# Probabilities scaled on ScalarE before the transposes, and value products in groups of four, in a fused two-block kernel

## The reference

```python
s = jnp.einsum('bqgrd,bqkgd->bqgrk', qg, kg).astype(jnp.float32) * scale
s = jnp.where(valid[:, :, None, None, :], s, -jnp.inf)
p = jax.nn.softmax(s, axis=-1).astype(v.dtype)
o = jnp.einsum('bqgrk,bqkgd->bqgrd', p, vg)
...
a = dsa_attention(q, k, v, qi, ki, wi, k_sel) * jax.nn.silu(z_a)
```

## Time and profile before

| what | us |
|---|---|
| median of the 3 runs | 3760.19 (3759.91 to 3761.3) |
| profiled execution, its own time | 3762.86 |
| its span in the trace | 3761.1 |
| first transposes of the stage | 1229.2 |
| last gate multiplication of the stage | 1679.03 |

### The profile page before, as it was taken

How to read it: one execution, slowest core, us unless ns; L and a number is a source line. 1 busy time by engine, 2 the same in 40 slices (tenths; PEclk the granted TensorE clock), 3 DMA queues, 4 the chain that set the end, 5 groups by cost and what they waited for, 6 DMA issues and landing times. The chain is left out here.

```text
span 3761.1 us, 43857 instructions
## 1 busy us (share of the span) xinstructions
PE 3273.5 (87%) x16134; PEld 2654.4 (71%) x16134; DVE 1837.2 (49%) x3636; ACT 1579.1 (42%) x2489; POOL 878.7 (23%) x608
## 2 busy tenths in 40 slices
PE   4995998859995899988797978996999999978799
PEld 3994777646774677757575866885888888856577
DVE  3773679998998665534232114662322132223223
ACT  2443668727891677750101113332544354421111
POOL 2551231120122000002322223332322222222122
PEclk9997999978997899996898988998999999989899
DMA  4565332242332311116543224546344644344422
GB/s 120 174 195 206 93 101 78 71 167 63 88 92 89 115 54 47 36 29 264 146 125 110 90 103 152 158 155 213 121 142 133 198 144 130 118 125 131 114 95 90
DMA packets 419811, 458.04 MB, mean 122 GB/s; under 512 B 30896, under 2 KB 301744, under 8 KB 417968
## 3 DMA queue, kind: packets, MB, share of 16 engines
q1 hardware_dynamic: 415888, 445.06, 38.3%
q10 hardware_dynamic: 3744, 10.65, 0.8%
HBM read 289.70 MB, written 165.94 MB: 121 GB/s over the span
## 5 line engine op out<-in xcount | busy, mean ns | idle before, releaser
L1220 PE MATMUL p_pr<-p_hT,p_w_hi 128*128 128x512 f32 x896 | 365.5, 408 | 101.2 <-POOL p_w_lo L990 33.5
L2336 PE MATMUL p_pr<-p_hT,p_w_hi 128*128 128x512 f32 x896 | 352.7, 394 | 17.0 <-DMA p_hT<-s_hT 17.0
L1161 DVE TENSOR_SCALAR_CACHE_REDUCE p_tied<-p_isc,p_level 128x1280 uint8<-128x1280 f32 (+9 forms) x276 | 359.8, 1357 | 3.1 <-DVE p_level L1154 0.4
L1221 PE MATMUL p_pr<-p_hT,p_w_hi 128*128 128x512 f32 x896 | 359.2, 401 | 0.0
L1222 PE MATMUL p_pr<-p_hT,p_w_lo 128*128 128x512 f32 x896 | 358.3, 400 | 0.0
L2337 PE MATMUL p_pr<-p_hT,p_w_hi 128*128 128x512 f32 x896 | 351.3, 392 | 0.0
L2338 PE MATMUL p_pr<-p_hT,p_w_lo 128*128 128x512 f32 x896 | 350.5, 391 | 0.0
L757 PE MATMUL t_pj_ps<-t_w_hi,t_hT_slot 128*128 128x356 f32 (+2 forms) x768 | 274.4, 357 | 39.9 <-POOL t_w_lo L473 25.4
L1107 ACT ACTIVATE p_junk_a<-p_isc,p_level 128x2048 int8<-128x2048 f32 (+5 forms) x192 | 276.4, 1441 | 34.3 <-DVE p_level L1176 31.4
L1845 PE MATMUL m_b_ps<-m_in_hi,m_w_hi 128*128 128x512 f32 x512 | 214.3, 419 | 77.2 <-POOL m_in_lo L1803 45.8
L1220 PEld LDWEIGHTS p_pr<-p_hT,p_w_hi 128*128 128x128 f32 x896 | 174.7, 195 | 151.0 <-issue 50.4
(11 more groups left out here) (269 smaller groups left out, 6958.5 us busy)
## 6 DMA issues: line engine op xcount, KB each, us to landing
p_w_raw<-in_w_in SPq DMA_DIRECT2D x112, 512.0 KB, 4.4
s_hT<-t_hT_slot SPq DMA_DIRECT2D x32, 1024.0 KB, 5.8
p_hT<-s_hT SPq DMA_DIRECT2D x64, 512.0 KB, 10.4
s_gT<-p_o_sb SPq DMA_DIRECT2D x128, 256.0 KB, 3.3
m_gates<-s_gT SPq DMA_DIRECT2D x64, 512.0 KB, 4.9
s_qT<-t_qT_slot SPq DMA_DIRECT2D x32, 512.0 KB, 2.7
s_zuT<-p_o_sb SPq DMA_DIRECT2D x64, 256.0 KB, 3.2
pl_wada<-in_w_ada SPq DMA_DIRECT2D x6, 2048.0 KB, 14.1
```

Source lines behind the costliest of these rows:

```text
L1161: return nc.vector.tensor_scalar(tied[:].bitcast(mybir.dt.uint8)[:, j:j + w], isc[:, o:o + w], level[:, b:b + 1], None, op, ALU.add, accum ...
L1220: nc.tensor.matmul(pr[slot][:], wh, hi, start=(k == 0), stop=False)
L1221: nc.tensor.matmul(pr[slot][:], wh, lo, start=False, stop=False)
L2336: nc.tensor.matmul(pr[n % NPR][:], wh, hi, start=(k == 0), stop=False)
```

## The change

- `spread_inverse`, `copy_inverse`, the multiplication by the inverse and the buffers `inv_t` and `o_sb` are gone. VectorE takes the reciprocal of each head by itself, and a new ScalarE step `normalise` multiplies the head's whole row of `prob` by it, in place, two steps after the head's last score piece. The first transposes of a turn wait for the four heads to be normalised. VectorE's `finish` is one multiplication by the gate.
- From tile 12 on, values are weighed in groups of four tiles (65 groups) and below that in pairs as before (6 groups).
- `AHEAD` goes from 4 to 8: the scores of a turn end 8 tiles before it starts. `pt` has 8 buffers for 6.

```diff
-    NS, NT, NPT, NPROB = 3, 3, 6, 3
+    NS, NT, NPT, NPROB = 3, 3, 8, 3
...
-    oi_ps = [ps(f"oi_ps{n}", [P, 2, PAIRS * P]) for n in range(2)]
+    o_ps = [ps(f"o_ps{n}", [P, PAIRS * P]) for n in range(2)]
...
-    AHEAD = 4
+    AHEAD = 8
     LAG = 2
+    PAIRED = 12
...
                 if m == len(pieces(i)) - 1:
-                    exps_at[step + 1 if turn >= 2 else 0].append((turn, r))
...
+                    exps_at[min(step + 1, KEYS[turn]) if turn >= 2 else 0].append((turn, r))
+                    inverts_at[min(step + 2, KEYS[turn]) if turn >= 2 else 0].append((turn, r))
...
     def weighed_at(n):
 
         m = n - LAG
-        return [m - 1, m] if n % 2 and m >= 1 else []
+        size = 2 if m < PAIRED else 4
+        return list(range(m - size + 1, m + 1)) if m >= 0 and m % size == size - 1 else []
...
-            def invert(turn):
-                dve.wait_ge(exped, REP * (turn + 1))
-                if turn >= 4:
-                    dve.wait_ge(inv_spread, turn - 3)
-                nc.vector.reciprocal(inv[:, turn % 4], total[:, turn % NPROB]).then_inc(inv_done, 1)
+            def invert(turn, r):
+                head = turn * REP + r
+                slot = head % (NPROB * REP)
+                dve.wait_ge(exped, head + 1)
+                if head >= NPROB * REP:
+                    dve.wait_ge(normed, head - NPROB * REP + 1)
+                nc.vector.reciprocal(inv[:, slot:slot + 1], total[:, slot:slot + 1]).then_inc(inv_done, 1)
...
-                dve.wait_ge(inv_copied, turn + 1)
-                if turn:
-                    dve.wait_ge(gated, turn)
-                nc.vector.tensor_tensor(o_sb[:], oi_ps[s][:, 0], inv_t[:, s], ALU.mult).then_inc(scaled, 1)
-                dve.wait_ge(scaled, turn + 1)
+                dve.wait_ge(weighed, KEYS[turn + 1])
...
-            def copy_inverse(turn):
-                s = turn % 2
-                act.wait_ge(inv_spread, turn + 1)
-                if turn >= 2:
-                    act.wait_ge(scaled, turn - 1)
-                nc.scalar.activation(inv_t[:, s], oi_ps[s][:, 1], ACT.Copy).then_inc(inv_copied, 1)
...
+            def normalise(turn, r):
+                n = (TURNS[turn][0] + 1) * P
+                head = turn * REP + r
+                slot = head % (NPROB * REP)
+                act.wait_ge(inv_done, head + 1)
+                nc.scalar.activation(prob[:, slot, 0:n], prob[:, slot, 0:n], ACT.Copy, scale=inv[:, slot:slot + 1]
+                                     ).then_inc(normed, 1)
+
+            for n in range(N_TILES):
+                for turn, r in EXPS_AT[n]:
+                    exponential(turn, r)
+                for turn, r in INVERTS_AT[n]:
+                    normalise(turn, r)
+                copy_keys(n)
...
-                    pe.wait_ge(exped, REP * (turn + 1))
+                    pe.wait_ge(normed, REP * (turn + 1))
...
-            def spread_inverse(turn):
...
-                last.then_inc(inv_spread, 1)
...
-                for turn in ended_at(n):
-                    spread_inverse(turn)
```

More of the change, by code:

```diff
@@ L1293, in phase_attention @@
     minus = sb("minus", [P, NPROB * REP], F32)
-    total = sb("total", [P, NPROB, REP], F32)
-    inv = sb("inv", [P, 4, REP], F32)
+    total = sb("total", [P, NPROB * REP], F32)
+    inv = sb("inv", [P, NPROB * REP], F32)
     pt = sb("pt", [P, NPT, REP, P], F32)
-    inv_t = sb("inv_t", [P, 2, PAIRS * P], F32)
-    o_sb = sb("o_sb", [P, PAIRS * P], F32)
     z = sb("z", [P, 2, PAIRS, P], F32)
@@ L1332, in feeding @@
         exps_at = [[] for _ in range(N_TILES + 1)]
+        inverts_at = [[] for _ in range(N_TILES + 1)]
         done = 0
@@ L1447, in finish @@
                     dve.wait_ge(stored[s], 16 * (turn // 2))
-                nc.vector.tensor_tensor(aT[:, s].rearrange("p c t -> p (c t)"), o_sb[:], z[:, s].rearrange("p c t -> p (c t)"),
+                nc.vector.tensor_tensor(aT[:, s].rearrange("p c t -> p (c t)"), o_ps[s][:], z[:, s].rearrange("p c t -> p (c t)"),
                                         ALU.mult).then_inc(gated, 1)
@@ L1454, in _ @@
                         scores(turn, r, m)
-                    turn, j = TILES[n]
-                    if j == min(1, TURNS[turn][0]):
-                        invert(turn)
+                    for turn, r in INVERTS_AT[n]:
+                        invert(turn, r)
                 if n:
@@ L1468, in exponential @@
                 act.wait_ge(negated, head + 1)
-                if turn >= NPROB and r == 0:
-                    act.wait_ge(inv_done, turn - NPROB + 1)
+                if turn >= NPROB:
+                    act.wait_ge(inv_done, head - NPROB * REP + 1)
                 nc.scalar.activation(prob[:, slot, 0:n], prob[:, slot, 0:n], ACT.Exp, bias=minus[:, slot:slot + 1],
-                                     scale=SCALE, accum_out=total[:, turn % NPROB, r:r + 1]).then_inc(exped, 1)
+                                     scale=SCALE, accum_out=total[:, slot:slot + 1]).then_inc(exped, 1)
             def copy_keys(n):
@@ L1532, in weigh @@
                 if j == 0 and turn >= 2:
-                    pe.wait_ge(scaled, turn - 1)
+                    pe.wait_ge(gated, turn - 1)
                 for half, p in ((0, slice(0, HD)), (1, slice(HD, P))):
-                    last = nc.tensor.matmul(oi_ps[turn % 2][p, 0], v[:, j, g, :], pt[:, n % NPT, half::2, :],
+                    last = nc.tensor.matmul(o_ps[turn % 2][p], v[:, j, g, :], pt[:, n % NPT, half::2, :],
                                             start=(j == 0), stop=(j == i))
                 last.then_inc(weighed, 1)
-            def spread_inverse(turn):
-                pe.wait_ge(inv_done, turn + 1)
-                if turn >= 2:
-                    pe.wait_ge(inv_copied, turn - 1)
-                for r in range(REP):
-                    p = slice(r % 2 * HD, (r % 2 + 1) * HD)
-                    last = nc.tensor.matmul(oi_ps[turn % 2][p, 1, r // 2 * P:(r // 2 + 1) * P],
-                                            inv[:, turn % 4, r:r + 1].to_broadcast([P, HD]), c.ident[:], start=True, stop=True)
-                last.then_inc(inv_spread, 1)
             for n in range(STEPS):
```

7 lines of the change are left out of this document (3 added, 4 removed).

## The result

The changed kernel takes 3776.3 us (median of 6 runs, 3773.1 to 3778.3) against 3761.0 us (3759.9 to 3769.2) of the kernel before beside it: ratio **1.0039**, 95% interval 1.0027 to 1.0051. That is 15.3 us slower; the forecast was 15.9 slower.

What follows compares the result with a forecast made beforehand. ScalarE would replace TensorE as the bound. First part +6, middle work +1.2, stalls +11 and last part -2.3 sum to +15.9 us on the median 3760.2, giving 3776; range 3756 to 3791.

Steps and rivals of the forecast that it cites:

- Busy shares: From 1300 to 1650: ScalarE busy 37 to 39 of 40 us, TensorE's weight loads with gaps of some 4.
- Price of the new operation: ScalarE's normalisation of 2048 columns would be recorded at 2.00 us and occupy ScalarE for 1.91.
- ScalarE's sum: Middle part, copy 12 to copy 247: exponentials, normalisations and copies total 377.1 us, 1.2 above the present 375.9.
- Stalls: Middle part: what ScalarE loses waiting, on top of its own work, +11 us, bounds 0 and 22.
- Early: Tiles 13 to 56: bunched scores delay transposes and ScalarE's copies wait, 6 us, about 3 at tile 26.
- the third rival: Much slower: waits let TensorE's granted clock drop, adding 15 to 25 us, 3790 to 3800; chance 0.10.
- Late: Above tile 150: ScalarE's copies wait for transposes, half of 25 groups losing 0.4 each, 5 us.
- First part: Up to copy 12: normalisations of turns 3 to 7 come on top, +6 us, between 0 and 10.6.
- Last part: From copy 247 to the last gate: TensorE leads again, 25.8 us against 28.2, -2.3.
- The saving comes through: Normalisations occupy ScalarE 1.0 us in the mean, not 1.32; TensorE stays the bound, 3728, partly to 3752; chance 0.12.
- The nearly even case: ScalarE-bound, but no operand price or smaller stalls and first part: 3756 to 3767; chance 0.18.
- groups of four save nothing: No changes of shape saved on TensorE: nothing altered in the middle part, 2 us in the last; no chance given.

Runs made afterwards that it cites:

- experiment 1: Changed kernel without the multiplication of the probabilities, so the output is not divided by the sums: 3728.8 us, 0.9912 of the kernel before.
- experiment 2: Changed kernel with each normalisation cut to the first 128 columns, all instructions and waits kept: 3734.4 us, 0.9929 of the kernel before.
- experiment 4: Changed kernel weighing values in pairs throughout in place of groups of four: 3778.9 us, 1.0047 of the kernel before.
- experiment 9: Changed kernel with `AHEAD` 4 and, from tile 12, VectorE's reciprocals ahead of the step's score pieces: 3757.2 us, 0.9995 of the kernel before.
- experiment 5: Changed kernel with `AHEAD` 4 in place of 8: 3767.6 us, 1.0016 of the kernel before.
- experiment 10: Experiment 9's kernel with the first head of each turn normalised on GpSimd in place of ScalarE: 3732.2 us, 0.9933 of the kernel before.
- experiment 6: Changed kernel with VectorE's reciprocals ahead of the same step's score pieces from tile 12 on: 3769.0 us, 1.002 of the kernel before.
- experiment 3: Kernel before with only groups of four from tile 12 and 8 pt buffers: 3750.1 us, 0.9972 of the kernel before.
- experiment 8: Kernel before with groups of four from tile 12, weighed one step later (`LAG` 3) with 10 pt buffers: 3749.1 us, 0.997 of the kernel before.

## Why the prediction came out right, and where it did not

The forecast that ScalarE becomes the bound and that its stalls are paid on top is confirmed by experiments 1, 2, 4 and 9. In its middle part two terms were off in opposite directions. Point by point:

**Busy shares: as forecast from 1340 on.** ScalarE 38.9 to 40 of 40 (37 to 39 said), TensorE's busy time 36.6 to 38.1. Not from 1300 to 1340, where ScalarE has 33.7. ScalarE's 25.4 us of idle time before copies lie within the 20 to 30 said: 7.8 up to copy 12, 8.2 from there to copy 57, 8.7 behind copy 247 and 0.7 between.

**Price of the new operation: right.** 2102 ns at 2048 against 2.00 us forecast, with an exponential now at 2101 for 2006. The occupancy is read from starts, ScalarE's timeline at a width of 1280:

```profile
1402.33 1.50 ACT L1469 ACTIVATE a_prob<-a_prob,a_minus 128x1280 f32<-128x1280 f32 x1
1403.58 0.33 ACT L1469 ACTIVATION_READ_ACCUMULATOR a_prob<-a_prob,a_minus 128x1 f32 x1
1403.67 0.73 ACT L1476 ACTIVATE a_pt<-a_t_ps 128x512 f32<-128x512 f32 x1
1404.15 1.50 ACT L1483 ACTIVATE a_prob<-a_prob,a_inv 128x1280 f32<-128x1280 f32 x1
1405.41 0.73 ACT L1476 ACTIVATE a_pt<-a_t_ps 128x512 f32<-128x512 f32 x1
```

The exponential holds ScalarE for 1.34 us, the normalisation for 1.26 and the copy for 0.48: 0.08 less for the one without a sum to read, where the prediction took 0.09.

**ScalarE's sum: too high.** 377.1 forecast, 372.1 by experiment 9 with the moved work put back. Each of some 427 operations in that part was priced about 0.01 us too dear. So the middle would be about 4 us shorter than before and not 1 longer, if nothing stalled.

**Stalls: too low.** With 372.1 of work in 390.1 us, 18.0 us are lost where the step said 11 (with its bounds at 0 and 22, though the range further on takes 18 as the upper one). The changed kernel's own trace records 16.0 of them as idle time, 8.9 before copies and 7.1 before normalisations. This is the term that was mis-sized, and it has two halves:

- *Early, about 10 for 6.* Tile 26, the example, went as drawn. TensorE, then ScalarE, in the changed kernel:

```profile
1307.90 1.51 PE L1532 MATMUL a_o_ps<-a_pt,a_v 128*64 128x256 f32 x12
1311.03 0.65 PE L1532 MATMUL a_o_ps<-a_pt,a_v 128*64 128x256 f32 x4 [1.62 <-ACT a_pt L1476]
1311.62 1.45 PE L1507 MATMUL a_s_ps<-a_kT,a_qT 128*128 128x512 f32 x6
1313.25 0.51 PE L1507 MATMUL a_s_ps<-a_kT,a_qT 128*128 128x256 f32 x2 [0.19 <-DVE a_tops L1418]
1313.60 0.60 PE L1519 MATMUL a_t_ps<-keep_ident,a_prob 128*128 128x128 f32 x4
```

```profile
1307.09 3.40 ACT L1483 ACTIVATE a_prob<-a_prob,a_inv 128x768 f32<-128x768 f32 x4
1310.40 1.54 ACT L1476 ACTIVATE a_pt<-a_t_ps 128x512 f32<-128x512 f32 x3
1314.23 0.60 ACT L1476 ACTIVATE a_pt<-a_t_ps 128x512 f32<-128x512 f32 x1 [2.29 <-PE a_t_ps L1519]
```

The last tile of the group waits for a copy behind four normalisations (1.62), four pieces are scored, and ScalarE stands for 2.29 us (3 said) until the transposes. Experiment 5 measures all such places together, about 10 us without the moved work (the trace records 9.3 as idle time: 1.87 before copy 13, 2.29 before copy 26, 3.57 before copy 38, 1.1 for reciprocals and little else). What the step left out is a part of the third rival:

```profile
1325.49 1.95 PE L1532 MATMUL a_o_ps<-a_pt,a_v 128*64 128x256 f32 x16
...
1332.95 1.11 PE L1519 MATMUL a_t_ps<-keep_ident,a_prob 128*128 128x128 f32 x4 [1.83 <-ACT a_pt L1476]
1333.99 3.68 PE L1532 MATMUL a_o_ps<-a_pt,a_v 128*64 128x256 f32 x16
1337.60 1.80 PE L1507 MATMUL a_s_ps<-a_kT,a_qT 128*128 128x512 f32 x4
1339.24 0.60 PE L1519 MATMUL a_t_ps<-keep_ident,a_prob 128*128 128x128 f32 x4
1339.60 1.06 PE L1507 MATMUL a_s_ps<-a_kT,a_qT 128*128 128x512 f32 x4
```

After waits for copies TensorE weighs its group in 3.68 us in place of 1.95, at the lower granted clock (1.2 GHz, half of the full one), and ScalarE stands idle for 3.57 us before its next copy. The stretch's clock is 0.91, and 1.00 in experiments 5, 9 and 10. From 1260 to 1300 it is 0.91 too, against 0.96 before, and from 1340 on 1.00 again, so the rival's 15 to 25 us did not come; how much of the 10 us was the clock and how much the order was not separated. The one wait behind the slow group is 3.57 us.

- *Late, the wrong wait.* The step lost 5 us to copies that wait for transposes above tile 150; there that wait was 0.4. In its place ScalarE waited for reciprocals, 7.1 us in the middle and 6.0 of them above tile 57, which experiment 6 takes away. The prediction said that VectorE hides 96 tiny reciprocals; it does hide their time, but not their place in its order.

**First part: 7.3 for 6** (copy 12 at 1283.5 for 1281, of which 1.3 was there when the stage began). Experiments 3 and 8, whose code is the same up to there but for a tile's delay in the weighing, differ by 6.2 in this part, so one profile doesn't measure it well. **Last part: -3.4 for -2.3.** In the tail without long operations ScalarE's copies come in step with TensorE's groups:

```profile
1680.86 2.07 ACT L1476 ACTIVATE a_pt<-a_t_ps 128x512 f32<-128x512 f32 x4 [1.75 <-PE a_t_ps L1519]
1684.67 2.07 ACT L1476 ACTIVATE a_pt<-a_t_ps 128x512 f32<-128x512 f32 x4 [1.74 <-PE a_t_ps L1519]
```

Four tiles in 3.81 us, against twice 2.04 before (1662.47 to 1664.51 of the earlier trace rows): 0.27 for each group saved, where 0.32 was taken. The step left out `AHEAD`: before, the last two pieces of scores and one exponential stand behind copy 247, and with `AHEAD` 8 they don't. Experiment 5, back at 4, gives 2.0 of the 3.4 back.

**The sum.** The stage's parts came to 19.4 us for 15.9; the program behind it, untouched, gave back 6.6 in that profile, and the medians differ by 15.3. That the total is met within 1 us is partly luck: the sum of ScalarE's work was 5 us too high and the stalls 7 too low, and the parts were 3.5 too low where the rest of the program gave back more than that.

**The rivals.** The saving comes through only without the new work (experiments 1 and 2) or with part of it elsewhere (10). The nearly even case is what experiment 9 is, the change with two orders mended. That groups of four save nothing is refuted by experiment 3.

**Left open in part.** Why groups of four alone give the kernel before 10 us and not 19. In the middle they give 9.2, and TensorE's new waits for VectorE in experiment 3 take 6.2. The two together are 15.4, near the 16.2 that 60 groups at the tail's 0.27 would make. This account is read from one trace, and no run tests it; experiment 1's 21.9 above tile 57 would then need more than 0.43 for a spreading.

## What to carry to other kernels

Work taken off the bounding engine is worth no more than the room that the receiving engine has left: add up the receiver's whole stage, start to start, before moving anything, and look for a third engine, even a slow one that is idle. An engine with free time can still delay others by the order of its instructions, so a tiny operation on which a full engine waits goes ahead of work that itself waits. When scores are produced ahead, spreading them over the steps matters more than producing them early: bunching cost 8 to 10 us in both kernels.

## What was not expected of the hardware

- **VectorE at 0.52 ns a column.** Its float32 multiplication by a per-row operand, SBUF to SBUF, took 1288 ns at 2048 and 286 at 128 (1002 ns for 1920 columns); ScalarE's exponential needs 0.84 for each (2006 - 401 over 1920) and GpSimd 2.52 (5442 - 608). The Trainium skill (VectorE: DVE Perf Modes, Mode 2×_2P — use both read ports for one tensor) says that an operation with a single tensor source in SBUF can yield two results a cycle. The rows agree: VectorE's reading of a score piece, with two sources and one of them in PSUM, takes 0.68 us for 512 columns and 0.42 for 256 in the changed kernel, 1.02 ns a column.
- **Recorded durations grow while an engine works without a break.** In the timeline at 1402 a copy is recorded with 0.73 us and the reading of a sum with 0.33, though the next instruction starts after 0.48 and 0.09; before, with ScalarE partly idle, a copy had 0.59. Behind an idle stretch a copy of the changed kernel is back at 0.60 (1314.23 above). Why they grow is not shown. On a full engine only the distance of starts is a price.
